# The second attention gate's row in two banks of the turned tiles

## The chip, the cores and the metric

The kernel runs on one core of a Trainium2 chip. The metric is the device time of one execution in microseconds (us); the numbers below are a median of three runs and one profiled execution.

## What is computed

A trunk of two layers over 1024 tokens of width 1024, in float32. Layer 0 is an mLSTM in chunks of 128 tokens with a squared-ReLU MLP (width 4096). Its result `h` gives one shared key and value: `kv = modulate(h, kv_shift, kv_scale) @ w_kv`, with 4 key heads of 64, and rotary positions on the keys' first 16 columns. Layer 1 is sliding-window attention (window 128, 16 query heads, a learned sink per head) with its own query projection, and a second MLP:

```
u = modulate(h, sh_m, sc_m)
q = rope_partial((u @ b_w_q[j]).reshape(B, S, A_HEADS, A_HEAD_DIM), positions)
y = swa_sink_attention(q, k_sh, v_sh, b_sinks[j]) @ b_w_o[j]
h = layer_norm(DEEPNORM_ALPHA * h + (1 + g_m) * y, ln_g[2 * layer], ln_b[2 * layer])
```

`g_m` is a vector of 1024 numbers for the whole layer, one of the six that a small projection of `c` gives. This case is about how `1 + g_m` of layer 1 is made into a row that stands in all 128 partitions (`gate_row`), so that VectorE can multiply the blocks of `b_w_o` by it while they are prepared.

## The kernel before

**Tiles and banks.** The tokens are eight tiles of 128 (`t` from 0 to 7). Each float32 product is made of three matmuls, high by high, high by low and low by high (L1775 to L1777); ScalarE makes the high part of a weight block (`whi`, L669), VectorE the low part (`wlo`, L1098). A group of 24 such matmuls over 512 columns fills one PSUM bank. The eight banks of PSUM are used so: banks 0 to 2 are a ring (`RING`) through which the groups go by their number modulo three, bank 3 (`M`) takes small things, banks 4 to 7 (`X` to `X + 3`) take the turned (transposed) tiles. `wait_evac` makes TensorE wait until the group three numbers before has been read out of its bank; the list that `group_engines` builds says for each group whether ScalarE ("A", counted in `act_evac`) or VectorE ("D", counted in `dve_evac`) reads it. `FIRST[name]` is a stage's first group.

**The order of work.** Each engine has its own program, written out by hand, and the engines wait for each other by semaphores; an engine takes its instructions strictly in that order. Nothing is planned at run time. The sync queue streams 512 KB blocks through the two places of `stage`, one when the block two before it has been used (`loads_used`).

**The key and value pass** lies between the first MLP and the queries. Its loop on TensorE (L2128 on) makes one group per key tile for `t` from 0 to 5 and the last two together (`last_two`, block by block, with two banks open, so that the first three weight blocks are given free early). Behind tile `t` come the transposes of the keys of tile `t - 2` (`k_transposed`, L2125, into bank `M`), which wait for the rotation of that tile and for ScalarE's copy of the one before (`evac_kt`, L929). Behind tile 5 stands `build_row` for the gate "gm1": it waits for the diagonal, and for each half for its ring bank, and multiplies a matrix of ones by the diagonal matrix in `acc` (L1831), one matmul in the source for each half, two in the trace. So the row's halves are two groups of the ring between key tile 5 and key tile 6.

**VectorE's loop** does for each `t`: the low parts of blocks 100 and 101 (at `t == 4`) or 102 and 103 (at `t == 6`); `take_keys(t)`, which copies values and keys out of the group's bank (L1598, L1579), rotates them (L1580 to L1582, the last of which gives the bank back) and finishes (L1587); `query_u(t)`, its half of the query input (L1531); `query_low(t - 2)` (L1550); and at `t == 4` `diagonal(G_M1)`, eight instructions that put `g_m` on the diagonal of `acc` (L1350). **ScalarE's loop** does at `t == 6` first `make_gate_row` (L845: read the two banks, add one, write `gate_row`), then the high parts of blocks 102 and 103, and for each `t` `evac_kt(t - 2)` (L929), its half of the query input (L815) and the high part of query tile `t - 1` (L824). **GpSimd** loads two rows of the layer norm, one of them into `acc`, once the row's groups are done (L604); ScalarE scales them later (L852). The key input's last turned tiles are copied out of banks 4 to 7 by ScalarE (L800, `tr_taken[0]`) and VectorE (L1539, `tr_taken[1]`) just as the pass begins. In the attention stage `turn_p` puts the turned probabilities into banks `X + 1` and `X + 2`.

Queries follow the pass on TensorE: a group for each of the tiles, with the last key transposes and the transposes of the queries between them.

Of the kernel before, what the change touches and what calls it, by code (L numbers as in the profile page):

```python
# [24 lines left out]
ACT = mybir.ActivationFunctionType  # L25

P = 128
S = 1024
D = 1024
DFF = 4 * D  # L30
T = S // P
K = D // P
HALF = 512
# [27 lines left out]
W_QK, W_V, W_O, W_OUT, W_MLP0 = 0, 8, 16, 24, 32  # L61
CHUNKS = DFF // HALF
W_KV = W_MLP0 + 8 * CHUNKS
W_Q = W_KV + 4
W_OP = W_Q + 8
# [111 lines left out]
def group_engines():  # L177

    out, first = "", {}

    def add(name, what):
        nonlocal out
        first[name] = len(out)
        out += what

    add("qk", "A" * 16)
    add("v", "D" * 16)
    add("o0", "A" * 8)
    add("o1a", "A" * 2)
    add("gm0", "A" * 2)  # L190
    add("o1b", "A" * 6)
    add("out0", "D" * 8)
    add("out1a", "D" * 4)
    add("gf0", "A" * 2)
    add("out1b", "D" * 4)
    add("mlp0", ("A" * 8 + "D" * 16) * CHUNKS)
    add("kva", "D" * 6)
    add("gm1", "A" * 2)
    add("kvb", "D" * 2)
    add("q", "".join("D" if kind == "q" else "A" for kind, _, _ in QUERY))  # L200
    add("op0", "D" * 8)
    add("op1a", "D" * 4)
    add("gf1", "A" * 2)
    add("op1b", "D" * 4)
    add("mlp1", ("A" * 8 + "D" * 16) * CHUNKS)
    return out, first


ENGINES, FIRST = group_engines()
# [16 lines left out]
def groups_through(w):  # L226

    for first, name in ((W_MLP0, "mlp0"), (W_MLP1, "mlp1")):
        if first <= w < first + 8 * CHUNKS:
            c, j = divmod(w - first, 8)  # L230
            return FIRST[name] + 24 * c + (UP.index((j, 1)) + 1 if j < 4 else 24)
    if w < W_V:
        return FIRST["qk"] + 2 * w + 2
    if W_Q <= w < W_OP:
        return QUERY_GROUP["q", (w - W_Q) // 4, T - 1] + 1
    for first, names in ((W_OP, ("op0", "op1b")), (W_KV, ("kvb", "kvb")), (W_OUT, ("out0", "out1b")),
                         (W_O, ("o0", "o1b")), (W_V, ("v", "v"))):
        if w >= first:
            second = (w - first) // 4
            size = {"v": T * (1 + second), "kvb": 2, "o1b": 6, "out1b": 4, "op1b": 4}  # L240
            return FIRST[names[second]] + size.get(names[second], T)


# [1 line left out]
TR_HS, TR_LN0, TR_KV, TR_LN2 = (T * i for i in range(4))  # L245
# [10 lines left out]
def build(nc, stream, early, xt, x, consts, out):  # L256
    ctx = ExitStack()

    def sb(name, shape, dt=F32, where=ctx):
        return where.enter_context(nc.sbuf_tensor(name, shape, dt))  # L260

    def sem(name):
        return ctx.enter_context(nc.semaphore(name))

    with ctx:
# [11 lines left out]
        acc = sb("acc", [P, D])  # L277
# [5 lines left out]
        ones = sb("ones", [P, 1])  # L283
# [11 lines left out]
        gate_row = sb("gate_row", [P, H * (DV + 1)])  # L295
# [39 lines left out]
        ps = ctx.enter_context(nc.psum_tensor("ps", [P, 8, HALF], F32))  # L335
        M = RING
        X = RING + 1
# [5 lines left out]
        early_in = [[sem(f"early_in{vec}_{k}") for k in range(K)] for vec in range(2)]  # L343
        mod_bias_in = sem("mod_bias_in")
        shift_sums = sem("shift_sums")
        quarters_done = sem("quarters_done")
        quarters_taken = sem("quarters_taken")
        first_mod = sem("first_mod")
# [6 lines left out]
        group_done = sem("group_done")  # L355
# [15 lines left out]
        diag_ready = sem("diag_ready")  # L371
# [22 lines left out]
        tr_taken = [sem("tr_taken0"), sem("tr_taken1")]  # L394
# [73 lines left out]
            return FIRST[name + "a"] + t if t < 4 else FIRST[name + "b"] + t - 4  # L468

        def kv_group(t):  # L470
            return FIRST["kva"] + t if t < 6 else FIRST["kvb"] + t - 6

        def gate_tanh(nh, t):

# [53 lines left out]
        def _(pool):  # L528
# [67 lines left out]
            for t in range(T):  # L596
                norm_scale(1, t)

            pool.wait_ge(group_done, FIRST["kva"])
            pool.dma_start(mask[:], consts["mask"]).then_inc(att_in, 16)  # L600
            pool.wait_ge(group_done, FIRST["gm1"] + 2)
            pool.wait_ge(h_written, T)
            for dst, src in ((lnrows[:, 1, :], "ln_g"), (acc[:], "ln_b")):
                pool.dma_start(dst, consts[src][1].partition_broadcast(P)).then_inc(rows_in, 16)  # L604
# [10 lines left out]
            for p in range(PAIRS):  # L615
                for r in range(2):
                    scale_probs(2 * p + r)
                t = p + 1 - T
# [28 lines left out]
        def _(act):  # L647
# [23 lines left out]
            def splits(*blocks):  # L671
                for w in blocks:
                    split(NUMBER["w", w], w)

            splits(0)
            for k in range(K):
                if k == 1:
# [4 lines left out]
                               bias=addv[:, 0, k:k + 1]).then_inc(u_made_by_act, 1)  # L682
# [128 lines left out]
            def query_u(t):  # L811

                act.wait_ge(kv_u[0], t + 1)
                for k in range(4):
                    last = act.activation(turned(t)[:, k, :], turned(t)[:, k, :], ACT.Identity,  # L815
                                          scale=mulv[:, 3, k:k + 1], bias=addv[:, 3, k:k + 1])
                last.then_inc(q_u[0], 1)

            def query_high(t):

                for j in range(2):
                    act.wait_ge(q_u[j], t + 1)
                act.wait_ge(group_done, kv_group(t) + 1)
                act.activation(uhi[:, :, t * P:(t + 1) * P], turned(t), ACT.Copy).then_inc(q_hi, 1)  # L824
# [16 lines left out]
            def make_gate_row(g):  # L841

                for half in range(2):
                    act.wait_ge(group_done, g + half + 1)
                    act.activation(gate_row[:, half * HALF:(half + 1) * HALF], ps[:, (g + half) % RING, :],  # L845
                                   ACT.Identity, bias=ones[:, 0:1]).then_inc(act_evac, 1)
# [80 lines left out]
            def evac_kt(t):  # L927
                act.wait_ge(kt_done, t + 1)
                act.activation(kt[:, :, t * P:(t + 1) * P],  # L929
                               ps[:, M, 0:2 * P].rearrange("p (m n) -> p m n", m=2), ACT.Copy).then_inc(kt_evac, 1)  # L930

            for t in range(T):
                if t == 6:
                    make_gate_row(FIRST["gm1"])
                if t in (4, T - 2):
                    splits(*((100, 101) if t == 4 else (102, 103)))
                if t >= 2:
                    evac_kt(t - 2)
                query_u(t)
                if t >= 1:  # L940
                    query_high(t - 1)
# [92 lines left out]
            for half in range(2):  # L1034
                part = resid[:, T - 1, half * HALF:(half + 1) * HALF]
                act.activation(part, part, ACT.Identity, scale=rstd[:, (T - 1) % 2, :],
                               bias=nmr[:, (T - 1) % 2, :]).then_inc(xhat_ready, 1)
# [3 lines left out]
        def _(v):  # L1041
# [59 lines left out]
            def preps(*blocks):  # L1101
                for w in blocks:
                    scale(NUMBER["w", w], w)
                    low(NUMBER["w", w], w)
# [257 lines left out]
            def gate_row_made(name):  # L1362
                v.wait_ge(act_evac, ACT_BEFORE[FIRST[name] + 2])
# [242 lines left out]
            for t in range(T):  # L1606
                if t in (4, T - 2):
                    preps(*((100, 101) if t == 4 else (102, 103)))
                if t:
                    take_keys(t)  # L1610
                query_u(t)
                if t >= 2:
                    query_low(t - 2)
                if t == 4:
                    diagonal(G_M1)
            query_low(T - 2)
            query_low(T - 1)
            gate_row_made("gm1")
            preps(104, 105)
            for t in range(T):  # L1620
                v.wait_ge(spilled[t], 16)
# [150 lines left out]
        def _(pe):  # L1772
# [53 lines left out]
            def build_row(g, n):  # L1826

                pe.wait_ge(diag_ready, n)
                for half in range(2):
                    wait_evac(pe, g + half)  # L1830
                    pe.matmul(ps[:, (g + half) % RING, :], ones[:, 0:1].to_broadcast([P, P]),  # L1831
                              acc[:, half * HALF:(half + 1) * HALF], start=True, stop=True).then_inc(group_done, 1)
# [91 lines left out]
            for k in range(K):  # L1924
                for half in range(2):
                    at = 32 * (k % 2 + 2 * half)
                    last = pe.matmul(ps[at:at + 32, X, :], gw[:, k, :], resid[:, k, half * HALF:(half + 1) * HALF],
                                     start=(k < 2), stop=(k >= K - 2))
# [18 lines left out]
            for j, r in enumerate((2, 4)):  # L1947
                last = pe.matmul(ps[0:1, M, j * HC:(j + 1) * HC], row[:, r, P - 1:P], ident[0:HC, 0:HC],
                                 start=True, stop=True)
# [5 lines left out]
                      stop=True).then_inc(gate_m, 1)  # L1955
# [3 lines left out]
            for j, src in enumerate((row[:, 3, :], winter[:], row[:, 5, :], row[:, 6, :])):  # L1959
                pe.transpose(ps[:, M, j * HC:(j + 1) * HC], src, ident[0:HC, 0:HC])  # L1960
            pe.matmul(ps[:, M, 4 * HC:5 * HC], winter[:, P - 1:P].to_broadcast([HC, P]), ident[0:HC, 0:HC],
                      start=True, stop=True).then_inc(gate_m, 1)
# [165 lines left out]
            for t in range(T):  # L2128
                if t < T - 2:
                    pe.wait_ge(ut_ready, 2 * (TR_KV + t) + 2)  # L2130
                    by_token(kv_group(t), W_KV, t)
                elif t == T - 2:
                    pe.wait_ge(ut_ready, 2 * (TR_KV + T))
                    last_two(kv_group(t), W_KV)
                if t == 1:
                    normed(TR_KV, 1, T - 1)
                if t == 5:
                    build_row(FIRST["gm1"], 3)
                if t >= 2:
                    k_transposed(t - 2)  # L2140

# [32 lines left out]
            def turn_p(n):  # L2174

                pe.wait_ge(p_scaled, n + 1)
                if n:
                    pe.wait_ge(p_taken, n)
                for j in range(1 if n // 2 % T == 0 else 0, 2):
                    for g in range(GROUP):  # L2180
                        last = pe.transpose(ps[:, X + 1 + j, g * P:(g + 1) * P],  # L2181
                                            probs_of(n)[:, g, j * P:(j + 1) * P], ident[:])
                last.then_inc(p_t, 1)
# [142 lines left out]
```

## Time and profile before

| | us |
|---|---|
| median of 3 runs | 2257.54 |
| lowest and highest run | 2256.47, 2257.54 |
| profiled execution, own time | 2254.4 |
| its span | 2252.3 |
| TensorE busy | 2202.0 (98%) |
| VectorE busy | 1237.4 (55%) |
| ScalarE busy | 703.8 (31%) |
| mean granted TensorE clock, share of full | 0.996 |

The span runs from the first to the last instruction that the profiler recorded; the execution's own time holds 2.1 us around it. The profile gives times from the span's start. A matmul's duration is the time from its start to its modelled end, and neighbours overlap, so the distance of two starts tells the cost: a timeline row of several instructions has the first one's start and the time to the last one's end. "Idle before" is the time in which the engine stood still ahead of a row, and the name behind the arrow is what ended it.

### The profile page before, as it was taken

How to read it: one execution, taken by the hardware profiler on the slowest of the kernel's cores; microseconds unless marked ns; L12 is line 12 of the kernel's file. 1: busy time of each engine (PE TensorE's matmuls, PEld its weight loads, DVE VectorE, ACT ScalarE, POOL GpSimd, SP SyncE). 2: the span in 40 equal slices, each digit the busy share in tenths (PEclk: the TensorE clock that was granted, in tenths of full speed). 3: DMA queues.
4: the chain of work that ended last, by engine and by line, in shares of the span. 5: the costliest groups of instructions: out<-in, count | busy, mean ns of one | idle time of the engine just before them, and what ended most of it. 6: DMA issues, size and time to landing. Idle time of an engine off the chain costs nothing.

```text
span 2252.3 us, 27958 instructions
## 1 busy us (share of the span) xinstructions
PE 2202.0 (98%) x10272; PEld 1788.0 (79%) x10272; DVE 1237.4 (55%) x2103; ACT 703.8 (31%) x1325; POOL 155.1 (7%) x201
## 2 busy tenths in 40 slices
PE   6999999999999999999998999999999999999998
PEld 5888888878888888888886866677888888888886
DVE  7424656587545545446576566757653453443446
ACT  4201544251311312202256355646131131121222
POOL 0000220010000000000010023321000000000004
PEclk9999999999999999999999999999999999999999
DMA  7434652223323224124221101111120120120211
GB/s 285 140 103 124 117 153 94 75 65 104 98 80 121 74 93 130 56 93 129 67 93 69 48 28 38 66 48 57 57 75 28 47 73 20 56 64 19 65 38 75
DMA packets 52431, 183.94 MB, mean 82 GB/s; under 512 B 7472, under 2 KB 7648, under 8 KB 52352
## 3 DMA queue, kind: packets, MB, share of 16 engines
q1 hardware_dynamic: 44640, 161.50, 22.3%
q0 software_dynamic: 4944, 16.96, 3.5%
q10 hardware_dynamic: 2768, 4.41, 0.5%
q8 instruction: 51, 0.84, 0.2%
q14 instruction: 28, 0.23, 0.0%
HBM read 174.43 MB, written 8.42 MB: 81 GB/s over the span
## 4 chain that ended last, share of the span: by engine, by line
PE 89%; DVE 6%; ACT 2%; issue 1%; DMA 1%; POOL 1%; SPq 0%; ACTq 0%; DVEq 0%
PE ps L1775 27%; PE ps L1777 27%; PE ps L1776 27%; PE ps L2169 1%; PE ps L2197 1%; PE ps L2181 1%; DVE wlo L1098 1%; ACT whi L669 1%; DMA early_place<-in_early 1%; PE ps L2019 1%; PE ps L1878 1%; PE ps L2004 1%; PE ps L2008 1%; DVE stats L1407 1%; DVE ulo L1382 1%
## 5 line engine op out<-in xcount | busy, mean ns | idle before, releaser
L1775 PE MATMUL ps<-uhi,whi 128*128 128x512 f32 x1152 | 450.5, 391 | 4.7 <-DVE wlo L1098 1.5
L1776 PE MATMUL ps<-ulo,whi 128*128 128x512 f32 x1152 | 448.5, 389 | 0.0
L1777 PE MATMUL ps<-uhi,wlo 128*128 128x512 f32 x1152 | 448.5, 389 | 0.0
L1775 PE MATMUL ps<-whi,hhi 128*128 128x512 f32 x1024 | 400.6, 391 | 0.0
L1777 PE MATMUL ps<-whi,hlo 128*128 128x512 f32 x1024 | 398.8, 389 | 0.0
L1776 PE MATMUL ps<-wlo,hhi 128*128 128x512 f32 x1024 | 398.6, 389 | 0.0
L1506 DVE TENSOR_TENSOR resid<-ps,resid 128x512 f32<-128x512 f32 x256 | 176.5, 690 | 348.3 <-PE ps L1777 338.4
L1775 PE MATMUL ps<-whi,uhi 128*128 128x512 f32 x704 | 288.3, 410 | 5.9 <-ACT gate_row L845 3.6
L1098 DVE TENSOR_TENSOR wlo<-stage,whi 128x1024 fp32r<-128x1024 f32 x180 | 220.3, 1228 | 118.6 <-ACT whi L669 118.3
L895 ACT ACTIVATE h_whole<-ps 128x512 f32<-128x512 f32 x128 | 76.4, 597 | 648.1 <-PE ps L1777 648.1
L1777 PE MATMUL ps<-whi,ulo 128*128 128x512 f32 x704 | 276.3, 392 | 0.0
L1776 PE MATMUL ps<-wlo,uhi 128*128 128x512 f32 x704 | 275.6, 392 | 0.0
L1775 PEld LDWEIGHTS ps<-uhi,whi 128*128 128x128 f32 x1152 | 216.3, 188 | 54.0 <-DVE wlo L1098 3.9
L1777 PEld LDWEIGHTS ps<-uhi,wlo 128*128 128x128 f32 x1152 | 216.3, 188 | 45.2
L1776 PEld LDWEIGHTS ps<-ulo,whi 128*128 128x128 f32 x1152 | 216.3, 188 | 44.3
L669 ACT ACTIVATE whi<-stage 128x1024 fp32r<-128x1024 f32 x180 | 188.8, 1053 | 183.0 <-DVE stage L1093 75.4
L1775 PEld LDWEIGHTS ps<-whi,hhi 128*128 128x128 f32 x1024 | 192.3, 188 | 42.1 <-issue 2.9
L1777 PEld LDWEIGHTS ps<-whi,hlo 128*128 128x128 f32 x1024 | 192.3, 188 | 40.2
L1776 PEld LDWEIGHTS ps<-wlo,hhi 128*128 128x128 f32 x1024 | 192.3, 188 | 39.4
L1485 DVE TENSOR_TENSOR h_whole<-h_whole 128x512 f32<-128x512 f32 x128 | 88.5, 691 | 220.4 <-ACT h_whole L895 220.4
L1775 PEld LDWEIGHTS ps<-whi,uhi 128*128 128x128 f32 x704 | 132.8, 189 | 42.4 <-issue 13.7
L1777 PEld LDWEIGHTS ps<-whi,ulo 128*128 128x128 f32 x704 | 132.7, 189 | 29.0
(248 smaller groups left out, 2019.7 us busy)
## 6 DMA issues: line engine op xcount, KB each, us to landing
stage<-in_stream SPq DMA_DIRECT2D x276, 512.0 KB, 3.5
aux<-in_early SPq DMA_DIRECT2D x8, 512.0 KB, 7.3
early_place<-in_early SPq DMA_DIRECT2D x8, 512.0 KB, 15.0
resid<-in_xt SPq DMA_DIRECT2D x8, 512.0 KB, 16.5
resid<-in_x POOLq DMA_DIRECT2D x8, 512.0 KB, 9.6
resid_dram<-resid ACTq DMA_DIRECT2D x8, 512.0 KB, 2.6
resid<-resid_dram POOLq DMA_DIRECT2D x8, 512.0 KB, 3.6
out<-resid SPq DMA_DIRECT2D x7, 512.0 KB, 2.6
```

Of the source, the lines that this page charges most:

```text
L669: act.activation(whi[:, slot_of(w), :], stage[:, n % 2, :], ACT.Copy).then_inc(hi_ready, 1)
L895: act.activation(h_whole[:, f, cut], ps[:, (first + u) % RING, :], ACT.Relu).then_inc(act_evac, 1)
L1098: v.tensor_tensor(wlo[:, slot_of(w), :], stage[:, n % 2, :], fr(whi[:, slot_of(w), :]), ALU.subtract).then_inc(loads_used, 1)
L1382: v.tensor_tensor(ulo[:, 4 * j:4 * j + 4, cut], u_whole[:, 4 * j:4 * j + 4, cut], fr(uhi[:, 4 * j:4 * j + 4, cut]), ALU.subtract).then_inc ...
L1407: return v.bn_stats(stats[:, t % 2, 6 * half:6 * half + 6], resid[:, t, half * HALF:(half + 1) * HALF])
L1485: v.tensor_tensor(q, q, q, ALU.mult).then_inc(relu_sq, 1)
L1506: v.tensor_tensor(dst, ps[:, g % RING, :], dst, ALU.add).then_inc(dve_evac, 1)
L1775: pe.matmul(dst, left_hi, right_hi, start=start, stop=False)
L1776: pe.matmul(dst, left_hi, right_lo, start=False, stop=False)
L1777: return pe.matmul(dst, left_lo, right_hi, start=False, stop=stop)
L1878: last = pe.transpose(ps[:, X + n % 4, k * P:(k + 1) * P], src[:, at:at + P], ident[:])
L2004: last = pe.matmul(ps[:, X + 2 + h % 2, 0:DV + 1], qk[:, c, (H + h) * P:(H + h + 1) * P], val, start=True, stop=(c == 0))
```

## The change

The row's two halves leave the ring. They are no longer groups; the key and value pass is one list of eight groups that VectorE reads. TensorE builds the row at the same place of its order, behind key tile 5, but into banks `X + 1` and `X + 2`, when the diagonal is ready and when all turned key tiles have been copied out; two semaphores of its own say that a half is made (`second_row`) and that it has been read (`second_row_taken`). ScalarE reads it at the same place of its order, at `t == 6`. VectorE makes the diagonal at `t == 2` in place of `t == 4`. GpSimd's loads of the norm rows wait for `second_row`, VectorE's wait behind the loop for `second_row_taken`, and so does the first `turn_p`. Since the ring counts two groups fewer, every later group's number falls by two and its bank changes with it.

```
-    add("kva", "D" * 6)
-    add("gm1", "A" * 2)
-    add("kvb", "D" * 2)
+    add("kv", "D" * T)
...
         def kv_group(t):
-            return FIRST["kva"] + t if t < 6 else FIRST["kvb"] + t - 6
+            return FIRST["kv"] + t
...
-            pool.wait_ge(group_done, FIRST["kva"])
+            pool.wait_ge(group_done, FIRST["kv"])
             pool.dma_start(mask[:], consts["mask"]).then_inc(att_in, 16)
-            pool.wait_ge(group_done, FIRST["gm1"] + 2)
+            pool.wait_ge(second_row, 2)
...
                 if t == 6:
-                    make_gate_row(FIRST["gm1"])
+                    for half in range(2):
+                        act.wait_ge(second_row, half + 1)
+                        act.activation(gate_row[:, half * HALF:(half + 1) * HALF], ps[:, X + 1 + half, :], ACT.Identity,
+                                       bias=ones[:, 0:1]).then_inc(second_row_taken, 1)
...
-                if t == 4:
+                if t == 2:
                     diagonal(G_M1)
             query_low(T - 2)
             query_low(T - 1)
-            gate_row_made("gm1")
+            v.wait_ge(second_row_taken, 2)
...
                 if t == 5:
-                    build_row(FIRST["gm1"], 3)
+                    pe.wait_ge(diag_ready, 3)
+                    for half in range(2):
+                        pe.wait_ge(tr_taken[half], TR_KV + T)
+                    for half in range(2):
+                        pe.matmul(ps[:, X + 1 + half, :], ones[:, 0:1].to_broadcast([P, P]),
+                                  acc[:, half * HALF:(half + 1) * HALF], start=True, stop=True).then_inc(second_row, 1)
...
                 pe.wait_ge(p_scaled, n + 1)
+                if n == 0:
+                    pe.wait_ge(second_row_taken, 2)
```

## Rows read from the trace of the kernel before

**Rows 1.** The page: busy us, share of the span, instructions; weight loads.

```profile
PE 2202.0 (98%) x10272; PEld 1788.0 (79%) x10272; DVE 1237.4 (55%) x2103; ACT 703.8 (31%) x1325; POOL 155.1 (7%) x201
...
stage<-in_stream SPq DMA_DIRECT2D x276, 512.0 KB, 3.5
```

**Rows 2.** TensorE's waits, 0 to 1250, then 1250 on: total, times, longest.

```profile
PE ps L1831 <- DVE acc L1350: 3.6, 1, 3.6
PE ps L1775 <- ACT gate_row L845: 3.6, 1, 3.6
...
PE ps L2125 <- ACT kt L929: 1.4, 2, 0.9
...
PE ps L1775 <- ACT resid L952: 2.2, 1, 2.2
```

**Rows 3.** Timeline of TensorE, key pass: start, us, what, idle before it.

```profile
1208.16 0.41 PE L2125 MATMUL ps<-ident,probs 128*128 128x128 f32 x2 [0.88 <-ACT kt L929]
...
1213.88 0.38 PE L2125 MATMUL ps<-ident,probs 128*128 128x128 f32 x2
1214.02 0.48 PE L1775 MATMUL ps<-whi,uhi 128*128 128x512 f32 x1
...
1219.37 0.39 PE L1777 MATMUL ps<-whi,ulo 128*128 128x512 f32 x1
1223.40 2.88 PE L1831 MATMUL ps<-acc,ones 128*128 128x512 f32 x4 [3.65 <-DVE acc L1350]
1226.07 0.64 PE L2125 MATMUL ps<-ident,probs 128*128 128x128 f32 x2
1230.32 0.77 PE L1775 MATMUL ps<-whi,uhi 128*128 128x512 f32 x1 [3.62 <-ACT gate_row L845]
...
1243.33 0.38 PE L2125 MATMUL ps<-ident,probs 128*128 128x128 f32 x2
1244.28 0.41 PE L2125 MATMUL ps<-ident,probs 128*128 128x128 f32 x2 [0.56 <-ACT kt L929]
1244.44 0.48 PE L1775 MATMUL ps<-whi,uhi 128*128 128x512 f32 x1
```

**Rows 4.** Windows, key pass: stretch, us, busy (instructions), clock, DMA share, GB/s.

```profile
1201.00:1219.60 18.60, 17.73 (x81) 13.97 (x79) 17.88 (x54) 15.19 (x31) 0.00 (x0) 1.00 0.08 24
1219.60:1223.40 3.80, 0.15 (x1) 0.00 (x0) 3.80 (x15) 0.00 (x0) 0.00 (x0) 1.00 0.47 164
1223.40:1226.30 2.90, 2.90 (x6) 1.28 (x6) 2.76 (x11) 0.00 (x0) 0.00 (x0) 0.67 0.00 0
1226.30:1230.30 4.00, 0.41 (x2) 0.01 (x2) 0.84 (x1) 3.56 (x8) 1.05 (x2) 0.50 0.59 217
1230.30:1234.50 4.20, 4.18 (x10) 3.33 (x11) 0.00 (x0) 0.45 (x1) 0.00 (x0) 0.50 0.12 43
```

**Rows 5.** Timeline of VectorE, steps 3 to 5 of its loop.

```profile
1210.71 1.21 DVE L1550 TENSOR_TENSOR ulo<-resid,uhi 128x1024 fp32r<-128x1024 f32 x1
...
1213.34 0.23 DVE L1587 TENSOR_TENSOR probs<-rtmp 128x64 f32<-128x64 f32 x1
...
1217.91 0.41 DVE L1598 COPY vv<-ps 128x256 f32<-128x256 f32 x1
...
1219.14 0.22 DVE L1582 TENSOR_TENSOR rtmp<-ps,rope 128x64 f32<-128x64 f32 x1
...
1221.70 1.65 DVE L1350 TENSOR_SCALAR acc<-ident,mods 128x128 f32<-128x128 f32 x8
1223.27 0.41 DVE L1598 COPY vv<-ps 128x256 f32<-128x256 f32 x1
```

**Rows 6.** Timeline of ScalarE, from the fourth key copy to the gate row.

```profile
1226.74 0.38 ACT L929 ACTIVATE kt<-ps 128x256 f32<-128x256 f32 x1 [8.83 <-PE ps L2125]
...
1229.51 1.24 ACT L845 ACTIVATE gate_row<-ps,ones 128x512 f32<-128x512 f32 x2
```

**Rows 7.** Chain of work that ended last, 1180 to 1300: start, us, what.

```profile
1229.60 0.58 ACT gate_row L845
```

**Rows 8.** Timelines of ScalarE and VectorE: last turned key tile copied.

```profile
1198.43 0.58 ACT L800 ACTIVATE resid<-ps 128x512 f32<-128x512 f32 x1
...
1201.21 0.68 DVE L1539 COPY resid<-ps 128x512 f32<-128x512 f32 x1
```

**Rows 9.** Timeline of TensorE: another gate's row; one key tile's 24 matmuls.

```profile
1512.51 1.88 PE L1831 MATMUL ps<-acc,ones 128*128 128x512 f32 x4
1514.22 1.04 PE L1878 MATMUL ps<-ident,resid 128*128 128x128 f32 x8
...
1195.78 0.47 PE L1775 MATMUL ps<-whi,uhi 128*128 128x512 f32 x1
...
1201.35 0.44 PE L2125 MATMUL ps<-ident,probs 128*128 128x128 f32 x2
```

**Rows 10.** Timelines of GpSimd and ScalarE: norm rows loaded and scaled.

```profile
1226.58 0.53 POOL L604 DMA_DIRECT2D lnrows<-in_ln_g  x1 [36.03 <-PE ps L1831]
...
1256.43 1.05 ACT L852 ACTIVATE lnrows<-lnrows 128x1024 f32<-128x1024 f32 x1
```

**Rows 11.** Windows, the second MLP.

```profile
1600.00:2000.00 400.00, 400.00 (x1766) 331.36 (x1765) 169.36 (x206) 77.15 (x104) 1.15 (x2) 1.00 0.15 47
```

More of the change, by code:

```diff
@@ L235, in groups_through @@
         return QUERY_GROUP["q", (w - W_Q) // 4, T - 1] + 1
-    for first, names in ((W_OP, ("op0", "op1b")), (W_KV, ("kvb", "kvb")), (W_OUT, ("out0", "out1b")),
+    for first, names in ((W_OP, ("op0", "op1b")), (W_KV, ("kv", "kv")), (W_OUT, ("out0", "out1b")),
                          (W_O, ("o0", "o1b")), (W_V, ("v", "v"))):
@@ L239, in groups_through @@
             second = (w - first) // 4
-            size = {"v": T * (1 + second), "kvb": 2, "o1b": 6, "out1b": 4, "op1b": 4}
+            size = {"v": T * (1 + second), "o1b": 6, "out1b": 4, "op1b": 4}
             return FIRST[names[second]] + size.get(names[second], T)
@@ L345, in build @@
         shift_sums = sem("shift_sums")
+        second_row = sem("second_row")
+        second_row_taken = sem("second_row_taken")
         quarters_done = sem("quarters_done")
```

## The prediction

> **What bounds the kernel now.** I read the page's busy times first: TensorE is busy for 98% of the span, VectorE for 55% [rows 1]. So a change of this kind can only take away time in which TensorE stands still, or TensorE time itself. The table of TensorE's waits comes next [rows 2]. Behind the start-up, its two longest are 3.6 us on the diagonal in acc (L1350) and 3.6 us on gate_row (L845). These are the two waits that the change is about. The third is kt (L929), 1.4 us in two pieces. The timeline of TensorE puts all of them into one stretch, the key and value pass [rows 3]. The last matmul of key tile 5 starts at 1219.37. The row's first matmul starts at 1223.40, the transposes behind the row at 1226.07, the last two key tiles at 1230.32. The windows add what the waits table can't show [rows 4]: the granted clock is 1.00 up to 1223.40, 0.67 in the row, and 0.50 until 1234.50, so the half level (1.2 GHz) also costs time in the matmuls.
>
> Why each stall is there is read from the other two engines. VectorE has no gap between 1210.71 and 1227, and the diagonal is its last piece of key step 4, 1221.70 to 1223.27 [rows 5]. ScalarE's gate row comes at 1229.51, behind kt (1226.74), the query input and its high part, and all of that can only start after TensorE's transposes behind the row [rows 6]. Key tile 7 shares a ring bank with the row's first half, and last_two waits for both of its banks before it starts.
>
> **The change, part by part.** All in the profiled execution's own time.
>
> (a) The diagonal goes from step 4 to step 2 of VectorE's loop. Its eight instructions take 1223.27 - 1221.70 = 1.57 us [rows 5]. It now runs behind the low part that starts at 1210.71, so from about 1211.85 to 1213.42. Everything of VectorE from there to the old diagonal moves back by 1.57, and what follows at 1223.27 stays, since the chain is gapless and its content the same. TensorE wants the diagonal at 1219.6, six microseconds later. First stall gone.
>
> (b) The row's banks. It also waits until both halves of the last turned key tile have been copied: 1198.43 + 0.58 on ScalarE and 1201.21 + 0.68 on VectorE [rows 8], some 18 us before the row can start. I cost the two added waits at nothing; the trace shows no such pair of satisfied waits alone. The bound below is nothing. Below nothing it can't go, since a wait only adds. The bound above is 0.14 us, the time from the end of gate_row's first half (1229.60 + 0.58 = 1230.18 in the chain of waits [rows 7]) to the matmul that it let go at 1230.32 [rows 3]. I take nothing, because the transposes at 1213.88 follow the last matmul before them without a gap though they stand behind two waits of the same kind.
>
> (c) TensorE without the stalls. Tile 5's last matmul starts at 1219.37 and the next instruction can start 0.23 later, 1219.60. The same row build at full clock takes 1514.22 - 1512.51 = 1.71 us [rows 9] against 1226.07 - 1223.40 = 2.67 here. Transposes at 1221.31; in the undisturbed step they take 1214.02 - 1213.88 = 0.14 [rows 3]. So last_two could start at 1221.45. It has three conditions. The transposes need the rotation of tile 3, which ends at 1213.34 + 0.23 [rows 5] and moves 1.57 back, to 1215.14. The ring now holds only key groups, so last_two waits for the banks of tiles 3 and 4. Tile 4's is given back by the third rotation instruction, which ends at 1219.36 and moves by 1.57 to 1220.93 [rows 5]; with 0.14 us of semaphore that is 1221.07. This is what is late next, and it misses being a wait by 0.38 us. The start is 1221.45 against 1230.32: 8.87 us gained.
>
> (d) The clock. With no standstill, the two tiles should run at the full level (2.4 GHz). They take 1243.33 - 1230.32 = 13.01 us now. One tile of 24 matmuls takes 1201.35 - 1195.78 = 5.57 at full clock [rows 9]; two in one run, with the switch from the transposes counted once, 5.57 + 24 x 0.227 = 11.02 (0.227 is 400.00 / 1766 [rows 11]). Gained: 1.99.
>
> (e) What is queued behind. ScalarE's gate row now needs only the row: 3.44 us after the transposes start (1229.51 - 1226.07), so at 1221.31 + 3.44 = 1224.8, and it ends 1.24 later, near 1226.0. Block 102's slot is free a quarter into last_two (1224.2), block 103's at half (1226.9), so their high parts are ready near 1228.2 and the low parts near 1229.5. TensorE wants block 103 in the query pass, which moves from 1244.44 to 1233.6, and there three quarters into the first tile, 1237.7: eight microseconds of slack. The sync queue's loads of 102 and 103 are issued up to 1.57 us later than before, since they wait for the low parts of 100 and 101 (the second ends by 1218.0 [rows 5], then by 1219.6), and with the page's 3.5 us from issue to landing [rows 1] they are in by 1223.1, before ScalarE asks at 1226.0. The GpSimd queue's two row loads now go at 1221.3 instead of 1226.58, and ScalarE uses them at 1256.43 [rows 10], which becomes 1245.6: free. VectorE's wait for the row's second half is long over when it comes. The wait added before the first turn of the probabilities stands behind the whole first query pass, the row's second half is copied at 1226: free. The kt wait of 0.56 us at 1244.28 stays, for its whole chain moves along.
>
> (f) Behind 1244 every engine waits for TensorE or for what TensorE releases, so all moves as one. Sum: 8.87 + 1.99 = 10.86, say 10.9 us. The profiled execution took 2254.4, span 2252.3; it would become 2243.5. The median of the three runs lies 3.1 above it, and I carry the difference over: 2257.54 - 10.9 = 2246.6 us. A measurement of this kernel tells about 0.2%, 4.5 us, from no change.
>
> **The clock, weighed.** Ahead of the stalls TensorE has small gaps too (the 0.88 us wait at 1208.16, the group ends), and the clock stays at 1.00 [rows 3, 4]; it falls only after it stood still for 3.65 us. The Trainium skill says in "TensorE: Matmul & The Clock Gate", section "A second HAM failure mode: psum-queue depth-cycling", that short idles between groups of matmuls that walk through PSUM banks can by themselves make the clock swing between its levels. By that rule the fall would come here without the long stall, and 10.9 would become 7.9; the trace speaks against it.
>
> **Rivals.**
> 1. *VectorE's chain takes over* (10%). The 0.38 us of margin in (c) is small, and the low parts of 100 and 101 stand in the same chain behind ScalarE's high parts. If tile 4 comes later by 1 to 3 us, last_two waits that much less the margin: 2247.2 to 2249.2. Against it: the parts moved are all in SBUF or long ready in PSUM.
> 2. *The clock falls all the same* (7%). Then the row costs 2.67 and last_two 13.01: 0.96 + 1.99 = 2.95 less; 2257.54 - 7.9 = 2249.6. For it: in the row's stretch the weight loads are busy for only 1.28 of 2.90 us [rows 4]. Against: the same row at 1512.51 shows the fast time [rows 9].
> 3. *Given back, or not there* (8%). Something later that doesn't move with TensorE eats most of it, or the row's wait for the turned tiles is released late. For it: TensorE's waits behind 1250 have a piece of 2.2 us on L952 [rows 2]. Against: that engine waits for TensorE in turn, and the streams have room (DMA share 0.15 between 1600 and 2000 [rows 11]). Price: most of 10.9; 2254 to 2258.
> 4. *Slower* (3%). Every later group changes its ring bank, since the ring counts two groups fewer: 242 groups (32 of queries, 18 of the output projection with its gate, 192 of the MLP). If the new place made a group dearer, for instance by meeting the scores' bank or a reader next to it, the loss grows with the number: from 10.9 / 242 = 45 ns a group it eats the gain, and at 65 ns the kernel takes 2257.5 - 10.9 + 15.7 = 2262.3, slower. Against: the ring passes through the same three banks in turn anyway, and 1600 to 2000 shows TensorE 400.00 busy with 1766 matmuls, 0.2265 each, whatever the bank [rows 11].
>
> **How the numbers follow.** The forecast as worked out has 72%, its own range 2245 to 2248. Rivals 1 and 2 (17%) reach to 2249.6. Rival 3 in its milder half begins at 2251. So the range is 2243.5 to 2250.5: below the forecast 3 us, for a median that carries less than 3.1 over the profiled run. Faster by over 0.2%: 72 + 10 + 7 = 89%. Within 0.2%: 8%. Slower: 3%.
>
> **What will show it.** The new row starts at about 1219.6 with no wait, takes 1.7, and last_two starts near 1221.5. The granted clock is 1.00 from 1201 to 1256. No wait on L1350 in this pass, none on gate_row. The first query group starts near 1233.6 and MLP and end are 10.9 earlier. Wrong if last_two shows a wait on VectorE, if the clock reads 0.50 anywhere there, or if the distance to before shrinks between 1244 and the end.

## The result and the profile after

The changed kernel takes 2243.15 us (median of 4 runs, 2242.10 to 2244.53) against 2257.01 for the kernel before (4 runs, 2254.31 to 2257.54). The ratio is 0.9944 with a 95% interval of 0.9933 to 0.9956, which is 9.9 to 15.1 us. The forecast was 2246.6 with a range of 2243.5 to 2250.5, from a kernel before at 2257.54. That base times the ratio gives 2244.9, inside the range; the plain median lies 0.35 us under its low end. The gain by the ratio is 12.6 us for a forecast 10.9. The profiled execution took 2242.1 us, span 2240.4, against 2254.4 and 2252.3.

The timeline of TensorE in the key and value pass of the changed kernel (start, duration, what; the row is now L2145, the key transposes L2128, the products L1778 to L1780). It answers to [rows 3]:

```profile
1207.47 0.41 PE L2128 MATMUL ps<-ident,probs 128*128 128x128 f32 x2 [0.89 <-ACT kt L929]
...
1213.20 0.38 PE L2128 MATMUL ps<-ident,probs 128*128 128x128 f32 x2
...
1218.67 0.39 PE L1780 MATMUL ps<-whi,ulo 128*128 128x512 f32 x1
1218.90 1.88 PE L2145 MATMUL ps<-acc,ones 128*128 128x512 f32 x4
1220.62 0.38 PE L2128 MATMUL ps<-ident,probs 128*128 128x128 f32 x2
1220.75 0.48 PE L1778 MATMUL ps<-whi,uhi 128*128 128x512 f32 x1
...
1231.77 0.38 PE L2128 MATMUL ps<-ident,probs 128*128 128x128 f32 x2
1232.72 0.41 PE L2128 MATMUL ps<-ident,probs 128*128 128x128 f32 x2 [0.56 <-ACT kt L929]
```

The first query group starts behind that, at 1232.88. The row follows tile 5 after 0.23 us, takes 1.72, and last_two takes 11.02. Neither long wait is left; the two short ones on kt are as they were. The whole pass is 0.7 us earlier than before already at 1207, because the execution reached it earlier; that is scatter of the start, as the repeats below show.

The windows of the same stretch of the changed kernel (us, busy of TensorE, its weight loads, VectorE, ScalarE, GpSimd, granted clock, DMA share, GB/s), to be held against [rows 4]:

```profile
1201.00:1218.90 17.90, 17.01 (x77) 13.74 (x77) 17.36 (x54) 14.84 (x30) 0.00 (x0) 1.00 0.02 3
1218.90:1220.70 1.80, 1.80 (x6) 0.79 (x5) 1.66 (x8) 0.00 (x0) 0.00 (x0) 1.00 0.84 271
1220.70:1231.80 11.10, 11.10 (x52) 9.13 (x51) 9.09 (x22) 6.04 (x10) 1.08 (x2) 1.00 0.65 213
```

The clock column reads 1.00 throughout. These are the two rows of VectorE's timeline on which steps (a) and (c) rest, and ScalarE's row for (e):

```profile
1211.14 1.66 DVE L1353 TENSOR_SCALAR acc<-ident,mods 128x128 f32<-128x128 f32 x8
...
1220.01 0.22 DVE L1585 TENSOR_TENSOR rtmp<-ps,rope 128x64 f32<-128x64 f32 x1
...
1223.81 1.25 ACT L936 ACTIVATE gate_row<-ps,ones 128x512 f32<-128x512 f32 x2
```

Tile 4's bank is given back at 1220.23; with 0.14 for the semaphore that is 0.38 us ahead of last_two at 1220.75.

**One yardstick for all runs.** The time from the transposes behind key tile 2 (1213.88 before, 1213.20 after) to the first matmul of the queries (1244.44 and 1232.88) holds all that the change touches, and leaves out the start and the rest. I call it the stretch: 30.56 us before, 19.68 after, 10.88 less. What lies behind it, to the end of the span, is 1007.9 before and 1007.5 after.

### The profile page after: what moved, and what is told of

Its sections match the earlier page's. It is cut to its first block, busy times and chain, and to the rows that moved or that the text cites. A ratio compares the mean times of both kernels' runs of the same rounds, so it can differ in the third digit from the quotient of the medians.

```text
span 2240.4 us, 27947 instructions
## 1 busy us (share of the span) xinstructions
PE 2201.3 (98%) x10272; PEld 1789.9 (80%) x10272; DVE 1236.7 (55%) x2103; ACT 703.9 (31%) x1325; POOL 154.7 (7%) x201
## 4 chain that ended last, share of the span: by engine, by line
PE 90%; DVE 5%; ACT 2%; issue 1%; DMA 1%; POOL 1%; SPq 0%; ACTq 0%; DVEq 0%
PE ps L1778 28%; PE ps L1780 27%; PE ps L1779 27%; PE ps L2177 1%; PE ps L2207 1%; PE ps L2191 1%; DVE wlo L1101 1%; ACT whi L669 1%; PE ps L2007 1%; PE ps L2022 1%; PE ps L1881 1%; DMA early_place<-in_early 1%; PE ps L2011 1%; DVE stats L1410 1%; DVE ulo L1385 1%
## 5 line engine op out<-in xcount | busy, mean ns | idle before, releaser
L1778 PE MATMUL ps<-uhi,whi 128*128 128x512 f32 x1152 | 450.6, 391 | 3.8 <-DVE ulo L1385 1.4
L1780 PE MATMUL ps<-uhi,wlo 128*128 128x512 f32 x1152 | 448.6, 389 | 0.0
L1778 PE MATMUL ps<-whi,hhi 128*128 128x512 f32 x1024 | 400.4, 391 | 0.0
L1780 PE MATMUL ps<-whi,hlo 128*128 128x512 f32 x1024 | 398.6, 389 | 0.0
L1778 PE MATMUL ps<-whi,uhi 128*128 128x512 f32 x704 | 288.2, 409 | 2.6 <-ACT resid L955 2.2
L1780 PE MATMUL ps<-whi,ulo 128*128 128x512 f32 x704 | 275.6, 392 | 0.0
L1778 PEld LDWEIGHTS ps<-uhi,whi 128*128 128x128 f32 x1152 | 216.5, 188 | 52.6 <-DVE wlo L1101 2.9
L1780 PEld LDWEIGHTS ps<-uhi,wlo 128*128 128x128 f32 x1152 | 216.4, 188 | 45.2
L1778 PEld LDWEIGHTS ps<-whi,hhi 128*128 128x128 f32 x1024 | 192.3, 188 | 42.2 <-issue 2.9
L1780 PEld LDWEIGHTS ps<-whi,hlo 128*128 128x128 f32 x1024 | 192.2, 188 | 40.2
L1778 PEld LDWEIGHTS ps<-whi,uhi 128*128 128x128 f32 x704 | 132.6, 188 | 38.8 <-issue 9.7
L1780 PEld LDWEIGHTS ps<-whi,ulo 128*128 128x128 f32 x704 | 132.5, 188 | 28.9
```

The source lines that it names most:

```text
L1778: pe.matmul(dst, left_hi, right_hi, start=start, stop=False)
L1780: return pe.matmul(dst, left_lo, right_hi, start=False, stop=stop)
```

## The experiments

| run | stretch, us | behind it, us | median, us | ratio to before, 95% |
|---|---|---|---|---|
| before, first profile | 30.56 | 1007.9 | 2257.01 | 1 |
| before, copy 1 | 31.58 | 1009.5 | 2257.06 | 1.0006 (0.9997 to 1.0015) |
| before, copies 2 and 3 | 31.82, 31.79 | 1009.6, 1009.6 | 2259.01, 2257.00 (one run each) | |
| changed, again | 19.69 | 1007.4 | 2242.98 | 0.9942 (0.9929 to 0.9956) |
| banks only | 26.62 | 1007.5 | 2248.36 | 0.9965 (0.9951 to 0.9979) |
| diagonal only | 26.98 | 1006.9 | 2249.08 | 0.9970 (0.9959 to 0.9982) |
| before, clock filled | 27.44 | 1006.9 | 2249.70 | 0.9973 (0.9963 to 0.9984) |
| changed, VectorE +8 | 21.03 | 1007.5 | 2244.27 | 0.9949 (0.9933 to 0.9964) |
| changed, VectorE +24 | 26.00 | 1007.7 | 2250.66 | 0.9976 (0.9965 to 0.9987) |
| changed, diagonal at 3 | 19.69 | 1006.8 | 2242.95 | 0.9942 (0.9929 to 0.9956) |
| kt earlier | 19.49 | 1007.4 | 2242.04 | 0.9940 (0.9927 to 0.9954) |
| kt earlier, diagonal ahead | 18.96 | 1007.8 | 2242.49 | 0.9946 (0.9932 to 0.9959) |

The kernel before had a median of 2255.75 beside the first four experiments (again, banks only, diagonal only, clock filled), 2255.06 beside the next four and 2255.04 beside the last two, copy 1 and the diagonal ahead. The stretch is that of one profiled execution; the median and the ratio come from all of a kernel's runs.

**The changed kernel again.**

> The changed kernel once more, so that its parts are compared with it on one chip. Theory (two waits in a row and the clock between them, 10.9 us in the key and value pass): 10.9 us under the kernel before, with last_two starting 8.9 us earlier relative to the last matmul of key tile 5 and no clock below 1.00 between that tile and the queries. The profile taken so far shows 11.9 in the span, 0.7 of it already there at key tile 5; if that 0.7 is only the start-up's scatter, it goes away or changes its sign here. Rival: the change also saves time ahead of the pass; then 0.7 shows up again.

The stretch is the same to 0.01 us. The 0.7 us ahead of the pass are gone: here the transposes behind tile 2 come at 1215.49, 2.3 later than in the first profile of the very same kernel. Scatter of the start, not a gain.

**Banks only.** The changed kernel with

```
-                if t == 2:
+                if t == 4:
                     diagonal(G_M1)
```

> Only the banks are changed, the diagonal stays at step 4. Theory: the first wait stays at 3.65 us, the row takes 2.67 with the clock falling, last_two follows the transposes without a wait at about +6.9 us behind tile 5's last matmul (10.95 in the kernel before, 2.1 in the changed one) and runs its first matmuls at the half clock, 13.0 us. So 4.0 us under before, 6.9 over the changed kernel. Rival (each half of the change carries its own wait and the clock costs belong to the second): 3.6 + 2.0 = 5.6 us under before. Rival (the banks carry nearly all): 9 us or more under before.

```profile
1222.04 3.78 PE L2145 MATMUL ps<-acc,ones 128*128 128x512 f32 x4 [3.65 <-DVE acc L1353]
1225.61 0.63 PE L2128 MATMUL ps<-ident,probs 128*128 128x128 f32 x2
1225.89 0.78 PE L1778 MATMUL ps<-whi,uhi 128*128 128x512 f32 x1
...
1238.03 0.38 PE L2128 MATMUL ps<-ident,probs 128*128 128x128 f32 x2
```

TensorE's timeline shows the first wait unchanged and none on the gate row; the stretch is 3.94 us shorter, 4.0 expected. The sum is nearer than its terms: the row takes 3.57 us at the half clock (2.67 expected) and last_two 12.14 (13.0 expected). The two rivals (5.6, 9 or more) are out by the trace: against full clock the row and last_two together still lose 1.85 + 1.12 = 2.97 us, as in the first profile of before, so the clock's cost did not go with the second wait. The measured times don't settle it: by the ratio the gain is 7.9 us (4.7 to 11.1), more than the stretch shows, which is taken up under the copies of before.

**Diagonal only.** The kernel before with its diagonal at step 2, the row in the ring.

> Only the diagonal moves to step 2, the row stays in the ring. Theory: the first wait goes, the row takes 1.7; but ScalarE reaches the gate row 3.4 us behind the transposes, so last_two still waits about 3.9 us on gate_row, starts about 6.1 us behind tile 5's last matmul, and the clock falls in this wait, 13.0 us for last_two. So 4.8 us under before. If the clock doesn't fall in a single wait of 3.9 us, 6.8. Rival (the diagonal is the root, and its delay is all that the second wait inherits): both waits go, 10 us or more under before.

```profile
1219.63 1.02 PE L1831 MATMUL ps<-acc,ones 128*128 128x512 f32 x2
1221.05 1.12 PE L1831 MATMUL ps<-acc,ones 128*128 128x512 f32 x2 [0.40 <-DVE rtmp L1582]
1222.01 0.38 PE L2125 MATMUL ps<-ident,probs 128*128 128x128 f32 x2
1226.01 0.77 PE L1775 MATMUL ps<-whi,uhi 128*128 128x512 f32 x1 [3.62 <-ACT gate_row L845]
...
1239.79 0.38 PE L2125 MATMUL ps<-ident,probs 128*128 128x128 f32 x2
```

The first wait is gone, the second stands at its full 3.62 us, because it is set by ScalarE's order behind the transposes and not by the diagonal. ScalarE reads the gate row 3.18 us behind the transposes here (1225.19 - 1222.01) and 3.44 in the kernel before. The stretch is 3.58 shorter, not 4.8. I had left out two things: the row's second half now waits 0.40 for tile 4's ring bank, which the moved diagonal made late, and last_two took 13.78 for an expected 13.0. The halves alone give 3.94 and 3.58, both together 10.88: each half takes away its own wait, but one long wait remains, and with it about 3 us of low clock.

**The clock by itself.** The kernel before, with

```
+                    keep_busy(15)
                     last_two(kv_group(t), W_KV)
...
                 if t == 5:
+                    pe.wait_ge(tr_taken[1], TR_KV + T)
+                    keep_busy(15)
                     build_row(FIRST["gm1"], 3)
```

> The kernel before with both waits in place, but TensorE turns an idle matrix 15 times (about 3.2 us at full clock) ahead of the row and again ahead of last_two, so that it isn't idle while it waits. Theory: the granted clock stays at 1.00, the row takes 1.7 in place of 2.7, last_two starts 0.96 earlier and takes 11.0 in place of 13.0: 2.95 us under before. Rival (the fall has another cause than standing still, or the slow matmuls come from something else): the clock row still shows 0.50 and nothing is gained, or the time grows by what the fillers overrun.

```profile
1218.91 3.51 PE L1824 MATMUL ps<-ident 128*128 128x128 f32 x30
1222.72 1.98 PE L1831 MATMUL ps<-acc,ones 128*128 128x512 f32 x4 [0.31 <-DVE acc L1350]
1224.54 0.38 PE L2125 MATMUL ps<-ident,probs 128*128 128x128 f32 x2
1224.76 3.51 PE L1824 MATMUL ps<-ident 128*128 128x128 f32 x30
1228.54 0.47 PE L1775 MATMUL ps<-whi,uhi 128*128 128x512 f32 x1 [0.27 <-ACT gate_row L845]
```

```profile
1218.90:1240.60 21.70, 20.56 (x118) 17.05 (x117) 11.99 (x36) 6.79 (x12) 1.05 (x2) 1.00 0.37 126
```

The work that the row waits for is as late as ever (the row starts 4.05 us behind tile 5's last matmul, 4.03 before), but the clock stays at 1.00, the row takes 1.82 us and last_two 10.98. The stretch is 3.12 shorter, against 2.95 expected: the clock's fall comes from the standstills, since it is gone when they are filled, and it costs about 3 us by the first profile of before.

**How near VectorE is.** The changed kernel with 8, then 24 more instructions of the diagonal's kind (the loop runs once, then three times):

```
                 if t == 2:
                     diagonal(G_M1)
+                    for _ in range(1):
+                        for k in range(K):
+                            ins = v.tensor_scalar(gate_row[:, k * P:(k + 1) * P], ident[:], mods[:, G_M1, k:k + 1], None,
+                                                  ALU.mult)
+                        step.mark(ins)
```

> The changed kernel with eight more instructions like the diagonal's behind it in VectorE's step 2 (written to the gate row's place, which is overwritten later; the result is the same). They delay tile 4's release of its bank by 1.6 us. Theory: the margin is 0.38 us, so last_two waits 1.2 us on VectorE, and the time is 1.2 over the changed kernel, with the clock at 1.00. Rival (VectorE has more room than that, as its 55% busy share says): no wait, same time.

```profile
1222.51 0.47 PE L1783 MATMUL ps<-whi,uhi 128*128 128x512 f32 x1 [1.11 <-DVE rtmp L1585]
```

> As the run with eight more instructions, but with 24, a delay of 4.8 us. Theory: last_two waits 4.4 us on VectorE, and standing still that long the clock falls to the half level as it did in the kernel before, which costs 2.0 more: 6.4 over the changed kernel, so only 4.5 under before. Rival: as for the eight, or the clock doesn't fall in this wait and it is 4.4 over.

```profile
1226.78 0.75 PE L1783 MATMUL ps<-whi,uhi 128*128 128x512 f32 x1 [4.48 <-DVE rtmp L1585]
```

```profile
1222.20:1226.70 4.50, 0.10 (x1) 0.00 (x0) 4.36 (x9) 2.60 (x6) 1.04 (x2) 1.00 0.65 204
1226.70:1233.00 6.30, 6.22 (x20) 5.05 (x21) 6.16 (x18) 3.27 (x4) 0.00 (x0) 0.73 0.47 187
```

The rows are last_two's first matmul in each, with what it waited for. The waits are 1.11 and 4.48 us (1.2 and 4.4 expected), the stretch grows by 1.35 and by 6.32 (1.2 and 6.4). In the larger dose two errors meet: last_two starts 4.74 us later (4.4 expected), and the clock costs it 1.58 (2.0 expected). So the margin of 0.38 us is real although VectorE is busy for 55% of the whole span. Behind 1.11 us of standing still the clock stays, behind 4.48 it falls: TensorE resumes at the half level, the clock in the second window reads 0.73, and last_two takes 12.60. Rival 1 of the prediction is a real mechanism; it begins once VectorE is more than 0.38 us later than in the changed kernel.

**The diagonal one step later.** `if t == 3:` in the changed kernel.

> The changed kernel with the diagonal at step 3 in place of 2. It is ready at about 1217 instead of 1213, still ahead of 1219.6, and tile 4's release is as late as before. Theory: same time as the changed kernel, within 0.3 us in the trace. Rival (step 2 is needed): a wait on the diagonal is back.

```profile
1215.32 1.65 DVE L1353 TENSOR_SCALAR acc<-ident,mods 128x128 f32<-128x128 f32 x8
```

The diagonal is ready near 1217.0, the row starts at 1219.29 without a wait, and the stretch is 19.69: step 2 isn't needed, step 3 does the same.

**The short waits.** The changed kernel, with k_transposed(T - 4) called behind the second block of last_two, and on ScalarE

```
-                if t >= 2:
+                if t >= 3:
                     evac_kt(t - 2)
                 query_u(t)
+                if t == 1:
+                    evac_kt(0)
```

> The changed kernel, and the two short waits on kt attacked too: ScalarE copies the first turned keys ahead of the high part of query tile 0, and TensorE puts the transposes of key tile 4 in the middle of last_two in place of behind it. Theory: the waits of 0.9 and 0.6 us with their semaphore times go, 1.5 us under the changed kernel, 12.4 under before. Rival: ScalarE or VectorE is then the one that is late in the same place (the high part of the query tiles comes later), and nothing is gained.

```profile
1207.20 0.41 PE L2132 MATMUL ps<-ident,probs 128*128 128x128 f32 x2
...
1221.07 0.47 PE L1780 MATMUL ps<-whi,uhi 128*128 128x512 f32 x1 [0.32 <-DVE rtmp L1587]
```

Both waits on kt are gone (the first lies ahead of the stretch: tile 0's transposes to tile 1's take 5.86 us in place of 6.80), but TensorE now arrives ahead of VectorE, and 0.32 us of a new wait stands in front of last_two. From tile 0's transposes to the queries it is 31.09 us against 32.21: 1.1 gained, 1.5 hoped for. The median is 0.9 under the changed kernel's in the first set and under the run with the diagonal at step 3 beside it (2242.95), and the intervals overlap: too small for the measured times, visible only in the trace. It has the lowest median of the versions tried, and is not shown to beat the changed kernel.

I then moved the diagonal out of the loop, in front of make_lo(TR_KV, T - 2):

> The kernel with kt copied earlier, and its diagonal made in a place where VectorE stood idle, 3.2 us waiting for ScalarE's high part behind the last key input but one, ahead of the loop. Theory (what is late next is VectorE's gapless chain through steps 0 to 4): the 0.32 us wait on VectorE ahead of last_two goes, so the stretch from the transposes behind key tile 2 to the first query group falls by 0.6 us to 18.9, and the time is 1.7 us under the changed kernel, 12.6 under before. Rival: the chain's later start shifts it by the diagonal's 1.57 us all the same (the idle time isn't free), the wait stays or grows.

```profile
1196.05 1.29 DVE L1387 TENSOR_TENSOR ulo<-u_whole,uhi 128x512 fp32r<-128x512 f32 x2 [3.15 <-ACT uhi L808]
...
1199.01 1.65 DVE L1355 TENSOR_SCALAR acc<-ident,mods 128x128 f32<-128x128 f32 x8
...
1203.89 0.44 PE L2131 MATMUL ps<-ident,probs 128*128 128x128 f32 x2 [1.03 <-DVE probs L1593]
```

The wait in front of last_two is gone and the stretch is 18.96, as expected (18.9). But the diagonal was put one piece too late, behind the idle time (3.15 us ahead of 1196.05) and not into it, so tile 0's rotation came late by it and TensorE waits 1.03 us there. That makes the hit on the stretch partly luck, because the wait moved ahead of where the stretch begins. Counted from the last key input's transposes, VectorE gives tile 4's bank back only 0.39 us earlier than in the version before, while TensorE, by its wait, comes 1.18 us later. From those transposes to the queries this version takes 38.11 us, the one before it 37.46, the changed kernel 38.58. So VectorE's chain did start later, by 1.18 of the diagonal's 1.57 us, as the rival said, and the median of 2242.49 is 0.5 to 0.7 us under the changed kernel's two, not 1.7. The place one step ahead of it wasn't tried.

**The kernel before, three more times.** By their medians, the runs with one part changed (banks only, diagonal only, clock filled) had gained 7.4, 6.7 and 6.1 us, which is 2.9 to 3.5 us more than their stretch shows against the first profile.

> The kernel before itself, unchanged. What is open: single changes measured 2 to 3 us more than their stretch of the trace shows. Theory (the clock's fall and return differ from run to run, and the start too): the ratio is 1.000 within its interval, but the profile shows another split, with the stretch from the transposes behind key tile 2 to the first query group at 30.6 us plus or minus 2. Rival: the arm of the kernel before is slow as such, and this copy measures about 1 to 2 us under it as well.

> The kernel before once more, for a second profile of the same stretch: 30.6 us plus or minus 2, by how long the half clock lasts.

> The kernel before once more, for a third profile of the same stretch: 30.6 us plus or minus 2, by how long the half clock lasts.

Copy 2's TensorE, timeline and windows; copies 1 and 3 read alike (row 3.57 and 3.58, last_two 13.11 and 13.33):

```profile
1225.03 3.78 PE L1831 MATMUL ps<-acc,ones 128*128 128x512 f32 x4 [3.65 <-DVE acc L1350]
1228.61 0.63 PE L2125 MATMUL ps<-ident,probs 128*128 128x128 f32 x2
1232.86 0.76 PE L1775 MATMUL ps<-whi,uhi 128*128 128x512 f32 x1 [3.62 <-ACT gate_row L845]
```

```profile
1221.20:1225.00 3.80, 0.18 (x1) 0.00 (x0) 3.80 (x15) 0.00 (x0) 0.00 (x0) 0.90 0.51 174
1225.00:1228.90 3.90, 3.87 (x6) 1.62 (x6) 3.64 (x11) 0.00 (x0) 0.00 (x0) 0.50 0.00 0
1228.90:1232.80 3.90, 0.34 (x2) 0.00 (x0) 0.00 (x0) 3.52 (x8) 1.05 (x2) 0.50 0.52 213
1232.80:1239.00 6.20, 6.14 (x17) 4.90 (x18) 0.00 (x0) 1.22 (x2) 0.00 (x0) 0.59 0.11 35
```

The waits are the same to 0.01 us in all four profiles; the clock is not. In the first profile it fell only during the row ([rows 4]: 0.67), in the copies it had fallen before the row began, and came back later behind 1232.8 as well. The stretch is 31.58, 31.82 and 31.79 us against 30.56, inside the 30.6 plus or minus 2 that was expected. The profile that I predicted from was the cheapest of four. The rival is not borne out: the copy measures the same as the kernel before beside it (1.0006, 0.9997 to 1.0015). Against the mean stretch of the four profiles, 31.44 us, banks only gains 4.8 us, diagonal only 4.5, clock filled 4.0 and the whole change 11.8.

The copies also take 1009.5 to 1009.6 us behind the stretch, and all other profiles 1006.8 to 1007.9; with the means of the four profiles, stretch and rest together give 6.5, 6.7 and 6.3 us for the three single changes, near the 7.4, 6.7 and 6.1 of their medians. The granted clock shows where: 160 us behind the first query group, where all of them wait 2.2 us on ScalarE's copy of a turned query tile. From the first query group to the end of that wait all 14 profiles take the same, to within 0.1 us. The windows are of copy 2, of the changed kernel, and of the one with the diagonal at step 3:

```profile
1400.00:1430.00 30.00, 26.42 (x146) 17.94 (x146) 21.73 (x64) 16.49 (x52) 8.70 (x6) 0.89 0.28 88
```

```profile
1390.00:1420.00 30.00, 27.75 (x157) 19.42 (x154) 23.97 (x69) 18.55 (x57) 11.10 (x8) 0.94 0.27 88
```

```profile
1390.00:1420.00 30.00, 27.05 (x164) 18.80 (x161) 24.57 (x70) 18.92 (x58) 11.36 (x8) 1.00 0.27 88
```

Same wait, three outcomes: the clock reads 0.89, 0.94 and 1.00, and the rest of the kernel takes 1009.6, 1007.5 and 1006.8 us.

## Why the prediction was right, and where its size was off

(a) and (b) held exactly: the diagonal ran behind the low part at 1211.14, and the row started 0.23 us behind tile 5's last matmul, with no cost for the added waits.

(c) held on its changed side to 0.01 us: 1220.75 - 1218.67 = 2.08 from tile 5's last matmul to last_two, 1221.45 - 1219.37 = 2.08 forecast. The margin that it named was tested with the two doses.

The clock's part is what was mis-sized: the 2.67 us of the row in (c) and the 13.01 us of last_two in (d). The changed side of (d) was right (11.02 forecast and measured); both figures of before were taken from one execution. Over the four profiles of before, row and last_two cost 3.35 and 13.20 us on average, so the clock's part is 1.63 + 2.18 = 3.8 us and not 2.95. Most of the difference is in the row. With it the stretch shrinks by 31.44 - 19.68 = 11.8 us. Nothing in the first profile's rows could show that. A range for the clock's part would have been due, since in the first profile the half level began inside the row, and it could as well have begun elsewhere. I took its cost as a constant.

(e) held: the gate row came 3.2 us behind the transposes (3.44 forecast, at the slower clock), and no wait of TensorE appeared on the weight blocks.

(f) held for the work and not for the clock: the first two profiled executions differ by 0.3 us behind the stretch, the copies of before by 2.1 from the changed kernel. With the four profiles' means, 11.8 in the stretch and about 1.6 behind it, the sum is 13.4 against 12.6 by the first ratio (interval 9.9 to 15.1). Whether the different clock at 1400 is a consequence of the shift or chance is open: three copies of before were at the half level longest there, about 7 us, one profile of before and seven of the ten others 3 to 4 us, three not at all. The mean granted clock of whole runs speaks for a consequence, without showing it. It is 0.992 to 0.994 in the three copies and 0.996 in the first profile of before. Of the 54 runs of the kernel before whose clock is on record, 35 read like the copies, and of the nine of the changed kernel none does (0.996 and 0.997).

One more term of (f) was off: the 3.1 us carried over from the profiled execution to the median. In the changed kernel the median lies only 1.05 above the profiled execution. So of the 3.45 us by which the median came out under the forecast, 2.05 are this term and 1.4 the profiled execution itself (2242.1 for 2243.5; 0.7 of that is the start, 0.3 lies behind the stretch and 0.4 outside the span). That median and profile of before were 3.1 us apart was already a sign that the profiled execution was a cheap one.

Rivals: 1 did not occur, last_two shows no wait on VectorE. 2 (the clock falls all the same) is refuted by the 1.00 in the windows: groups walk through the ring with gaps of up to 0.9 us and the clock stays, also with 1.11 us in front of last_two. What the Trainium skill's "TensorE: Matmul & The Clock Gate", section "A second HAM failure mode: psum-queue depth-cycling", reports of another kernel, a clock that swings by short idles between groups, is not seen in this stretch. 3 (given back) did not occur: what lies behind the stretch is 0.3 us shorter, not longer. 4 (dearer ring banks) is refuted too: 1600 to 2000 shows 1767 matmuls in 400.00 us, 1766 before.

## What to carry to other kernels

Where two long waits follow each other, price them together. Here each half of the change took away its own wait and gained 3.6 to 3.9 us of the stretch by itself, and both together 10.9, because either wait alone was enough to keep the low clock. Count the clock as a part of the price of a long standstill of TensorE, and give it a range from several profiles, since here its length changed from run to run while the waits didn't. And where an engine with a low average share has a gapless chain in one stretch, its margin there (0.38 us here) decides what the next improvement can bring.

## What had not been expected of the hardware

Around a standstill of 2.25 us in the attention stage, shorter than the 3.65 us of the key pass, the granted clock also falls to the half level, in 11 of 14 profiles. It falls between 0.3 us before and 1.5 us after the wait ends, for a time that differs from one execution to the next, and costs up to 2.8 us (1009.6 - 1006.8). No run took this wait away, and ahead of it TensorE runs small matmuls with a further wait of 0.7 us, so it is not shown that the standstill alone is the cause. In the key pass the waits repeat within 0.01 us, and the cost of the low clock behind them ranges from 2.95 to 4.2 us over four executions of one kernel (row and last_two above their 1.72 and 11.02 us at full clock).
